# A scalar operand moved from a shared scratch tensor to a tensor of its own

## The chip, the cores and the metric

The kernel runs on one core of a Trainium2 chip. The metric is the device time of one execution in microseconds (us). A core has five engines that run side by side: TensorE (PE, with its weight loads listed apart as PEld), VectorE (DVE), ScalarE (ACT), GpSimd (POOL) and SyncE (SP, which here issues the weight transfers and the stores of the output).

## The reference, cut to what matters

The model is a trunk of two layers over 256 tokens of width 2048, all in float32. Every layer ends both of its halves with a layer norm of a weighted residual, so there are four such norms, and the last of them is the output:

```
def _layernorm(x, w, b):
    mu = jnp.mean(xf, axis=-1, keepdims=True)
    var = jnp.mean(jnp.square(xf - mu), axis=-1, keepdims=True)
    y = (xf - mu) * lax.rsqrt(var + LN_EPS)
    return (y * w + b).astype(x.dtype)
...
for layer in range(2):
    mixed = rwkv7_time_mix(h) if layer == 0 else moba_attention(h)
    h = _layernorm(ALPHA * h + mixed, ln1_w[layer], ln1_b[layer])
    h = _layernorm(ALPHA * h + _swiglu(h, ...), ln2_w[layer], ln2_b[layer])
    if layer == 0:
        k_pad, v_pad, k_mean = _shared_kv(h, kv_w_k, kv_w_v)
return h
```

The reciprocal square root of each norm is what the change touches.

## The kernel before, in words

**Matrix products.** Each float32 weight matrix is streamed from memory in chunks of 256 x 512 values into a ring of four slots, `raw` (SyncE, L296). ScalarE rounds a chunk to `whi` (L950), VectorE writes the rest, `raw - whi`, to `wlo` (L1236, and L1509 in the projections that end in a residual). The activations are held as such a pair too: `ahi` and `alo`, or `hThi` and `hTlo` in the down projections. TensorE makes three products for each piece, at L494 to L496 and in the last block of a projection at L519 to L521: the activation piece (128 x 128) is the stationary operand that is loaded as weights, and the chunk of the ring is the moving one.

**The layer norms.** 256 tokens are two tiles of 128, t = 0 and t = 1. A projection that ends in a residual (`wo`, `down0`, `ao`, `down1`) is made in four blocks of 512 columns. In its last block TensorE finishes tile 0 first, so that VectorE can norm tile 0 while TensorE does tile 1. The function `last_block` does this for one tile: it adds the residual (L1530), takes the block's statistics (L1539), joins those of the four blocks to mean and variance in `mv` (L1540), and makes the reciprocal square root in `rstd` with a first guess from the bits of the float and three Newton steps. All of this works on one value for each token, [128, 1] operands: `x`, the variance plus epsilon, in `var`; `hx`, minus half of it; `y0`, the guess, in `rstd`; and `q`, a scratch value. Before the change both `q` and `hx` are columns of one scratch tensor, `small` of 32 columns: `q` is column t, `hx` is column 2 + t. A `then(...)` around an instruction makes VectorE wait until it has completed. The instruction that writes `hx` (L1543) has no such wait behind it; it signals `split_done` instead, except in the last norm. `hx` is read three times, as the second of the two [128, 1] scalars of L1550.

Eight tiles go through `last_block`: two in each of four norms. After it, `centred` subtracts the mean and multiplies with `rstd` (L1556), and TensorE transposes the result (L842) as the input of the next projection, whose first three chunks it makes at once from the unsplit weights (L852). In the last norm VectorE does the rest itself (L1671, L1676), and SyncE stores each block of 512 columns of the output (L353).

**Where tensors lie.** The tensors are placed in a partition's memory one after another in the order of their declarations, each start rounded up to a multiple of 32 bytes. `raw` starts at byte 16512, `whi`, `wlo`, `ident`, `mixT`, `lnT`, `stats`, `mv`, `var`, `rstd` follow, and `small` starts at byte 67360 with 128 bytes. Behind it come `gsm`, `nsmall`, `idle`, then `ahi` (and under the same bytes `a2t`) at 67904, `alo` at 84288, `big` at 100672 (and under the same bytes `common`, then `hThi` and `hTlo`), and at the end `bsum` and `asm`. `rec` in the profile is `rec2`, which lies under `whi` and `wlo`. Within `big`, the recurrence's tile `XS` starts 96 bytes behind a multiple of 64, since the small tile `PC` of 96 bytes is placed ahead of it; the neighbouring tiles `XT` start at multiples of 64.

Of the kernel before, what the change touches and what calls it, by code (L numbers as in the profile page):

```python
# [29 lines left out]
P = 128  # L30
D = 2048
T = 256
TT = T // P
# [96 lines left out]
def trunk(nc, x, rows, rwkv_rows, lora, w, consts, ln_rows, y):  # L130
    with ExitStack() as ctx:
# [3 lines left out]
        def sb(name, shape, dt=F32, stack=ctx):  # L135
            return stack.enter_context(nc.sbuf_tensor(name, shape, dt))
# [12 lines left out]
        var = sb("var", [P, TT])  # L149
        rstd = sb("rstd", [P, TT])  # L150
        small = sb("small", [P, 32])
        gsm = sb("gsm", [P, 5, 8])
        nsmall = sb("nsmall", [P, 48])
        idle = sb("idle", [P, 10])
# [1049 lines left out]
        def _(dve):  # L1204
# [3 lines left out]
            def then(ins):  # L1208

                step.up(ins)  # L1210
                dve.wait_ge(dve_step, step.now())
# [310 lines left out]
            def last_block(c0, kt, n, t):  # L1522

                c_next = c0 + NJ * kt // KC
                cs = slice((NJ - 1) * NB, NJ * NB)
                if t == 0:
                    dve.wait_ge(tile_done, n + 1)
                else:
                    dve.wait_ge(chunk_used, c_next)
                ins = V.scalar_tensor_tensor(out=Zn[:, t, cs], in0=H[:, t, cs], scalar=ALPHA, in1=ps[:, 2 + t, :], op0=ALU.mult, op1=ALU.add)  # L1530
                if t == 0 and c_next == CHUNKS:
                    then(ins)
                elif t == 0:
                    ins.then_inc(split_done, 1)
                    dve.wait_ge(split_done, c_next + 1)
                else:
                    ins.then_inc(bank_free[1], 1)
                    dve.wait_ge(bank_free[1], (c_jobs[n] + NJ - 1) // 2 + 2)
                then(V.bn_stats(stats[:, t, NJ - 1, :], Zn[:, t, cs]))  # L1539
                then(V.bn_aggr(mv[:, t, :], stats[:, t]))  # L1540
                I32 = mybir.dt.int32
                x, hx, y0, q = (m[:, t:t + 1] for m in (var, small[:, TT:2 * TT], rstd, small))
                ins = V.tensor_scalar(hx, mv[:, t, 1:2], LN_EPS, -0.5, ALU.add, ALU.mult)  # L1543
                if c_next < CHUNKS:
                    ins.then_inc(split_done, 1)
                then(V.tensor_scalar(x, mv[:, t, 1:2], LN_EPS, None, ALU.add))
                then(V.tensor_scalar(q.bitcast(I32), x.bitcast(I32), 1, None, ALU.logical_shift_right))
                then(V.tensor_scalar(y0.bitcast(I32), q.bitcast(I32), -1.0, float(0x5F3759DF), ALU.mult, ALU.add))
                for _ in range(3):
                    then(V.tensor_scalar(q, y0, y0, hx, ALU.mult, ALU.mult))  # L1550
                    then(V.scalar_tensor_tensor(out=y0, in0=q, scalar=1.5, in1=y0, op0=ALU.add, op1=ALU.mult))
# [13 lines left out]
            def norm(n, c_prev, kt, c0):  # L1565

                for t in range(TT):
                    last_block(c_prev, kt, n, t)
                    for b in range(NJ):
                        centred(t, b)  # L1570
                split_act(n, PLAIN)
                split_lo(c0 + PLAIN, 1, PLAIN)
                for g in range(PLAIN + 1, CJ):
                    split_act(n, g)
                split_lo(c0 + RING, 1)
                dve.wait_ge(chunk_used, c0 + PLAIN)
                for g in range(PLAIN):
                    split_act(n, g)
# [88 lines left out]
            for t in range(TT):  # L1667
                last_block(PH["down1"][0], FT, 3, t)
                for b in range(NJ):
                    cs = slice(b * NB, (b + 1) * NB)  # L1670
                    V.scalar_tensor_tensor(out=Zn[:, t, cs], in0=Zn[:, t, cs], scalar=mv[:, t, 0:1], in1=wb_last[:, 0, cs],  # L1671
                                           op0=ALU.subtract, op1=ALU.mult).then_inc(xhat_done, 1)
                for b in range(NJ):
                    cs = slice(b * NB, (b + 1) * NB)
                    dve.wait_ge(xhat_done, (3 * TT + t) * NJ + b + 1)
                    V.scalar_tensor_tensor(out=H[:, t, cs], in0=Zn[:, t, cs], scalar=rstd[:, t:t + 1], in1=wb_last[:, 1, cs],  # L1676
                                           op0=ALU.mult, op1=ALU.add).then_inc(h_done, 1)
# [31 lines left out]
```

## Time and profile before

| | us |
|---|---|
| median of 3 runs (2677.53 to 2678.38) | 2677.69 |
| the profiled execution | 2677.53 |
| span of its profile | 2675.7 |
| what lies around the span | 1.83 |

The profile is that of one execution. Busy times are sums over an engine's instructions; a chain of waits is the work that ended last, followed back from the end. A row of a group of instructions gives its line in the kernel, the engine, the operation, the tensor that is written and those that are read, the shapes, the count, the busy time with the mean of one in ns, and the idle time before them.

### The profile page before, as it was taken

To read this page: it belongs to the slowest core of one execution; us is meant where nothing else is said; L and a number is where in the kernel's file an instruction comes from. 1 tells how busy PE (TensorE), PEld (TensorE's weight loads), DVE (VectorE), ACT (ScalarE), POOL (GpSimd) and SP (SyncE) were. 2 spreads that over 40 slices of the span, in tenths; PEclk is the share of its full clock that TensorE was granted. 3 is DMA by queue.
4 is the path that set the end of the run, shared out by engine and by line. 5 is a ranking of instruction groups with operands and counts; after the bars stand their busy time and mean duration, and the time that the engine had idled before them with its cause. 6 is when DMAs were issued, how large, how long until landed. Compare 5 with 4: busy or idle time off the path is not lost.

```text
span 2675.7 us, 39424 instructions
## 1 busy us (share of the span) xinstructions
PE 2507.8 (94%) x15342; PEld 2045.2 (76%) x15342; DVE 1446.1 (54%) x1738; ACT 1086.0 (41%) x1326; POOL 139.3 (5%) x187
## 2 busy tenths in 40 slices
PE   7999968878999999999999999969999999999997
PEld 5877757766788888887888788857788888887886
DVE  4555976665664444444445644454754444444455
ACT  3444435432444444443333444443444444443332
POOL 1000024430000000000000000010000000000000
PEclk9999979889999999999999999989999999999999
DMA  5555710044466666665665666614566666666664
GB/s 176 166 172 167 216 29 8 14 137 145 150 199 189 186 189 187 188 185 160 191 194 178 210 190 191 193 55 143 155 197 188 188 188 184 189 185 194 191 190 133
DMA packets 219155, 440.75 MB, mean 165 GB/s; under 512 B 13216, under 2 KB 13248, under 8 KB 217824
## 3 DMA queue, kind: packets, MB, share of 16 engines
q1 hardware_dynamic: 214400, 413.19, 51.5%
q0 software_dynamic: 4640, 25.92, 3.5%
q8 instruction: 85, 1.39, 0.2%
q14 instruction: 30, 0.25, 0.0%
HBM read 436.96 MB, written 2.10 MB: 164 GB/s over the span
## 4 chain that ended last, share of the span: by engine, by line
PE 85%; DVE 9%; issue 2%; ACT 2%; DMA 1%; POOL 1%; DVEq 0%; ACTq 0%; POOLq 0%
PE ps L494 25%; PE ps L496 25%; PE ps L495 25%; DVE wlo L1236 2%; PE ps L694 1%; PE ps L880 1%; PE ps L684 1%; PE ps L704 1%; PE ps L852 1%; PE ps L581 1%; DVE rec L1376 1%; DVE alo L1563 1%; DMA big<-lora_a 1%; PE ps L599 1%; PE ps L588 1%
## 5 line engine op out<-in xcount | busy, mean ns | idle before, releaser
L950 ACT CAST whi<-raw 128x1024 fp32r<-128x1024 f32 x772 | 809.3, 1050 | 1234.4 <-PE ps L496 1159.6
L1236 DVE TENSOR_TENSOR wlo<-raw,whi 128x1024 fp32r<-128x1024 f32 x551 | 672.3, 1226 | 676.6 <-ACT whi L950 676.0
L494 PE MATMUL ps<-whi,ahi 128*128 128x512 f32 x2364 | 937.1, 396 | 29.0 <-DVE wlo L1236 12.5
L496 PE MATMUL ps<-whi,alo 128*128 128x512 f32 x2364 | 928.7, 393 | 0.0
L495 PE MATMUL ps<-wlo,ahi 128*128 128x512 f32 x2364 | 925.3, 391 | 0.0
L494 PEld LDWEIGHTS ps<-whi,ahi 128*128 128x128 f32 x2364 | 446.3, 189 | 130.2 <-issue 35.3
L496 PEld LDWEIGHTS ps<-whi,alo 128*128 128x128 f32 x2364 | 445.9, 189 | 101.9
L495 PEld LDWEIGHTS ps<-wlo,ahi 128*128 128x128 f32 x2364 | 446.1, 189 | 97.2 <-issue 0.7
L1509 DVE TENSOR_TENSOR wlo<-raw,whi 128x1024 fp32r<-128x1024 f32 x224 | 274.0, 1224 | 321.4 <-ACT whi L950 321.3
L494 PE MATMUL ps<-whi,hThi 128*128 128x512 f32 x672 | 264.4, 393 | 5.1 <-DVE hTlo L1613 5.1
L495 PE MATMUL ps<-wlo,hThi 128*128 128x512 f32 x672 | 266.0, 396 | 0.0
L496 PE MATMUL ps<-whi,hTlo 128*128 128x512 f32 x672 | 264.6, 394 | 0.0
L494 PEld LDWEIGHTS ps<-whi,hThi 128*128 128x128 f32 x672 | 127.5, 190 | 35.1 <-issue 5.8
L495 PEld LDWEIGHTS ps<-wlo,hThi 128*128 128x128 f32 x672 | 127.5, 190 | 27.6
L496 PEld LDWEIGHTS ps<-whi,hTlo 128*128 128x128 f32 x672 | 127.4, 190 | 27.1
L1126 ACT ACTIVATE a2t<-ps,lnT 128x128 f32<-128x128 f32 x96 | 34.2, 495 | 33.5 <-PE ps L842 33.5
L449 POOL DMA_DIRECT2D big<-ln_rows x3 | 1.7, 573 | 856.7 <-PE ps L521 836.2
L1376 DVE TENSOR_TENSOR rec<-ps,big 128x512 f32<-128x512 f32 x40 | 27.6, 690 | 33.5 <-PE ps L684 32.8
L1250 DVE SCALAR_TENSOR_TENSOR big<-big,mixT 128x256 f32<-128x256 f32 x96 | 40.0, 482 | 0.7
L1382 DVE STREAM_TRANSPOSE rec<-ps 128x512 f32<-128x512 f32 x32 | 22.9, 715 | 31.4 <-PE ps L694 30.9
L1613 DVE TENSOR_TENSOR hTlo<-ps,hThi 128x1024 f32 (+1 forms) x22 | 26.9, 1225 | 21.1 <-ACT hThi L1145 21.1
L694 PE MATMUL ps<-big,rec 64*64 64x64 f32 x960 | 32.7, 234 | 4.7 <-DVE rec L1376 3.9
(286 smaller groups left out, 1669.1 us busy)
## 6 DMA issues: line engine op xcount, KB each, us to landing
raw<-w_gate SPq DMA_DIRECT2D x176, 512.0 KB, 3.7
raw<-w_up SPq DMA_DIRECT2D x176, 512.0 KB, 3.7
raw<-w_down SPq DMA_DIRECT2D x176, 512.0 KB, 3.7
raw<-w_k SPq DMA_DIRECT2D x32, 512.0 KB, 4.2
raw<-w_r SPq DMA_DIRECT2D x32, 512.0 KB, 4.2
raw<-w_v SPq DMA_DIRECT2D x32, 512.0 KB, 4.5
raw<-w_o SPq DMA_DIRECT2D x32, 512.0 KB, 4.4
raw<-kv_k SPq DMA_DIRECT2D x32, 512.0 KB, 4.4
```

Source lines behind the costliest of these rows:

```text
L494: mm(o, hi[:, k, tok], whi[:, s, k2, :], start=(k == 0), stop=False)
L495: mm(o, hi[:, k, tok], wlo[:, s, k2, :], start=False, stop=False)
L496: last = mm(o, lo[:, k, tok], whi[:, s, k2, :], start=False, stop=(k == kt - 1))
L581: last = mm(ps[0:LR, 4 + n, 0:T], m[:, k, :], mx[:, k, :], start=(k == 0), stop=(k == KT - 1))
L694: quarters(lambda j, h, t, a, u, v: mm(ps[u, 2 + a, half(j)], Z[v, a, half(j)], XS[v, half(j)] if a else XT[g % 2][v, 0, half(j)], start=T ...
L950: nc.scalar.copy(whi[:, s], raw[:, s]).then_inc(hi_done, 1)
L1126: ins = A(hF[:, k, t * P:(t + 1) * P], ps[:, 4 + b, k2 * P:(k2 + 1) * P], ACT.Identity, scale=lnT[:, (n * 2) * KT + k:(n * 2) * KT + k + 1 ...
L1236: V.tensor_tensor(wlo[:, s], raw[:, s], whi[:, s].bitcast(F32), ALU.subtract).then_inc(split_done, 1)
L1250: return V.scalar_tensor_tensor(out=out, in0=xxT[:, k], scalar=mixT[:, m * KT + k:m * KT + k + 1], in1=xT[:, k, 1:T + 1], op0=ALU.mult, op ...
L1376: V.tensor_tensor(Z.rearrange("p l (j c) -> p l j c", c=CHUNK), ps[:, 0:2, 0:4 * CHUNK].rearrange("p l (j c) -> p l j c", c=CHUNK), mask_l ...
L1509: V.tensor_tensor(wlo[:, s], raw[:, s], whi[:, s].bitcast(F32), ALU.subtract).then_inc(split_done, 1)
L1613: V.tensor_tensor(hTlo[:, f0, :], ps[:, 4:6, :].rearrange("p a (k t) -> p (a k) t", k=2), hThi[:, f0, :].bitcast(F32), ALU.subtract).then_ ...
```

## The change

One tensor of two columns, `half_var`, is declared behind `small`, and `hx` becomes a column of it instead of column 2 + t of `small`. No instruction is added, taken away or reordered, and no wait changes. `half_var` has 8 bytes and so takes 32: it lies at byte 67488, where `gsm` was, and each tensor declared behind it starts 32 bytes later.

```diff
         small = sb("small", [P, 32])
+        half_var = sb("half_var", [P, TT])
         gsm = sb("gsm", [P, 5, 8])
...
-                x, hx, y0, q = (m[:, t:t + 1] for m in (var, small[:, TT:2 * TT], rstd, small))
+                x, hx, y0, q = (m[:, t:t + 1] for m in (var, half_var, rstd, small))
```

## Rows read from the trace of the kernel before

**Rows 1.** The page: shares of the chain of work that ended last.

```profile
PE 85%; DVE 9%; issue 2%; ACT 2%; DMA 1%; POOL 1%; DVEq 0%; ACTq 0%; POOLq 0%
```

**Rows 2.** Stretches: length; each engine's busy us (instructions); TensorE clock, DMA share, GB/s.

```profile
735.00:1490.00 755.00, 745.64 (x3276) 607.65 (x3276) 379.57 (x347) 307.12 (x317) 1.07 (x2) 0.99 0.63 187
2650.00:2675.70 25.70, 9.37 (x41) 7.34 (x40) 18.40 (x43) 0.00 (x0) 0.00 (x0) 0.74 0.24 82
```

**Rows 3.** The chain of waits in the last 20 us: first and last of six such pieces.

```profile
2656.36 0.28 DVE small L1550
...
2666.55 0.28 DVE small L1550
```

**Rows 4.** VectorE in order of time, last tile of last norm: start us, length us.

```profile
2664.91 0.15 DVE L1543 TENSOR_SCALAR small<-mv 128x1 f32<-128x1 f32 x1
2664.99 0.14 DVE L1546 TENSOR_SCALAR var<-mv 128x1 f32<-128x1 f32 x1
2665.16 0.15 DVE L1547 TENSOR_SCALAR small<-var 128x1 int32<-128x1 int32 x1
2665.35 0.15 DVE L1548 TENSOR_SCALAR rstd<-small 128x1 int32<-128x1 int32 x1
```

**Rows 5.** VectorE in order of time in the first norm, `centred` of both tiles.

```profile
711.28 1.92 DVE L1556 TENSOR_SCALAR common<-common,mv,rstd 128x512 f32<-128x512 f32 x4
...
717.00 1.92 DVE L1556 TENSOR_SCALAR common<-common,mv,rstd 128x512 f32<-128x512 f32 x4
```

**Rows 6.** The chain of waits there: start us, length us, what.

```profile
712.85 1.75 PE ps L842 x16
...
714.93 5.39 PE ps L852 x12
720.32 0.45 PE ps L842 x4
```

**Rows 7.** VectorE's groups of instructions, shapes kept apart.

```profile
L1550 DVE TENSOR_SCALAR small<-rstd,small 128x1 f32<-128x1 f32 x24 | 6.6, 273 | 0.9
L1547 DVE TENSOR_SCALAR small<-var 128x1 int32<-128x1 int32 x8 | 1.2, 154 | 0.3
L1556 DVE TENSOR_SCALAR common<-common,mv,rstd 128x512 f32<-128x512 f32 x24 | 11.5, 543 | 0.2
L1562 DVE CAST ahi<-a2t 128x512 fp32r<-128x512 f32 x24 | 10.1, 421 | 14.5 <-ACT a2t L1126 14.5
```

**Rows 8.** The page: TensorE's weight loads at line 494.

```profile
L494 PEld LDWEIGHTS ps<-whi,ahi 128*128 128x128 f32 x2364 | 446.3, 189 | 130.2 <-issue 35.3
...
L494 PEld LDWEIGHTS ps<-whi,hThi 128*128 128x128 f32 x672 | 127.5, 190 | 35.1 <-issue 5.8
```

**Rows 9.** Line 694, products on `XS` and `XT`: ns min/median/max, first and last start.

```profile
L694 PE MATMUL ps<-big,rec x960: 213/218/366, 381.0 to 577.0; 64*64 64x64 f32 x192
L694 PE MATMUL ps<-rec x320: 216/218/366, 381.0 to 557.7; 64*64 64x64 f32 x160
```

**Rows 10.** ScalarE's copies into `XS` (L1036) and `XT` (L1043).

```profile
L1036 ACT COPY big<-ps 64x256 f32<-64x256 f32 x32 | 11.8, 370 | 0.4
L1043 ACT COPY rec<-ps 128x256 f32<-128x256 f32 x16 | 6.0, 373 | 25.4 <-DVE rec L1382 25.4
```

**Rows 11.** Line 1250, reading `xT` at steps of 1028 bytes.

```profile
L1250 DVE SCALAR_TENSOR_TENSOR big<-big,mixT x96: 475/480/491, 17.7 to 265.2; 128x256 f32<-128x256 f32 x96
```

**Rows 12.** The chain of waits, whole span: its two transfers among the longest pieces.

```profile
7.05 14.12 DMA big<-lora_a
...
266.55 7.31 DMA big<-rwkv_rows
```

**Rows 13.** Page: DMA queues: packets, MB, share of 16 engines.

```profile
q1 hardware_dynamic: 214400, 413.19, 51.5%
q0 software_dynamic: 4640, 25.92, 3.5%
```

**Rows 14.** The output's stores, from the answer on their tensor.

```profile
DMA to landing us min/median/max: 2.4/2.7/2.8
```

## The prediction

> **What bounds the kernel now.** I read the page first. The chain of work that ended last is TensorE for 85% of the span and VectorE for 9% [rows 1], so a change on VectorE counts only where the chain runs through it. Next the stretches. In 735 to 1490 us, products without a norm between them, TensorE is busy for 745.64 of 755 us with 3276 products, 228 ns each, and VectorE for half of the time [rows 2]. There nothing that VectorE does for 0.1 us is seen. The last 25.7 us are the opposite: TensorE works for 9.37 us in them and VectorE for 18.40. The chain of waits shows why: it runs through L1550 six times, three Newton steps for each of the two tiles of the last norm [rows 3]. In the three other norms the same instructions have a cover. In the first norm, tile 0's `centred` starts at 711.28 and its first of four pieces is done after a quarter of 1.92 us, at 711.76 [rows 5]; TensorE turns to it only at 712.85, when it has finished tile 1 [rows 6], so 1.09 us are free. Tile 1's first piece is done at 717.48 [rows 5], and TensorE takes it at 720.32, behind the 12 products of L852 [rows 6]: 2.84 us are free. The reader is to see that of eight passes through `last_block` only two lie on the path.
>
> **The change part by part.** Nothing is added or removed: the same instructions on the same engines, in the same order, with the same waits, semaphores and transfers. What changes is addresses, of two sorts. I cost every one of them at nothing, and bound each from the rows.
>
> (a) *Where `hx` lies, as it is read.* L1550 reads `y0` as its tensor, `y0` again as its first scalar and `hx` as its second, and writes `q`. It takes 273 ns, where L1547, of the same size with a constant in place of the scalars, takes 154 [rows 7]: 119 ns more. Before the change `hx` lies in the tensor that L1550 writes, 8 bytes from the value. Is the 119 ns the price of that closeness? L1556 says no: it reads two [128, 1] scalars, `mv` and `rstd`, neither of which lies in the tensor that it writes, and takes 543 ns, where the cast of L1562, which has the same 512 values a partition and no scalar, takes 421 [rows 7]. That is 122 ns more. So two scalars cost about 120 ns wherever they lie; 122 - 119 = 3 ns is what the closeness could be worth, and in six instructions on the path that is 0.02 us. Expected: nothing. Bounds: if in spite of that row the closeness were the whole price, moving `hx` away would give back 6 x 0.119 = 0.71 us on the path, and 24 x 0.119 = 2.86 us if none of the 24 had a cover. In the other direction a further scalar's price, half of 119 ns, six times, is a loss of 0.36 us; if the pair's price doubled, it would be 0.71 us and 2.86 us in the same way.
>
> The Trainium skill (Advanced Engine Details and Errata, SBUF Cachelines) speaks against this change: it gives lines of 16 bytes, with full speed when following accesses hit the same line and a penalty when they don't. The four values of `q` and `hx` fill just one such line before (byte 67360 is 4210 x 16) and two after. By that rule L1550 would get slower, and the time would be that of the rival of a dearer L1550 below.
>
> (b) *Where `hx` lies, as it is written.* L1543 has no wait behind it, and L1546 starts 0.08 us after it, although it lasts 0.15; where a wait stands between, the next instruction starts after 0.19 (L1547 to L1548) [rows 4]. Both orders write different tensors before and after, so I expect the same. If the new address held L1546 back, each pass would lose 0.11 us, 0.22 us on the path for two passes and 0.88 for eight. If the cover of (a) and (b) were gone in all eight, the sum would be 3.74 us, still only 0.14%.
>
> (c) *The shift by 32 bytes.* This is the part with reach. `ahi`, `alo`, `hThi` and `hTlo`, all of `big` and `common` start at multiples of 64 before, and 32 bytes beyond one after. The ring `raw`, `whi`, `wlo` lies ahead of `small` and stays, and with it the moving operand of nearly all products, ScalarE's L950 and VectorE's L1236 and L1509. What moves is TensorE's stationary operand. Its load takes 189 ns from `ahi` and 190 from `hThi` [rows 8] and lies beside the 228 ns of a product, so it has 38 ns to grow in before any product is late. Rows on operands that are 32 bytes off already: `XS` is read as the moving operand at L694, and 640 of the 960 products of the group `big` read it, the other 320 `XT`; the median of this group is 218 ns, like that of the group `rec`, which reads only `XT` at multiples of 64 [rows 9]. ScalarE writes 256 values into `XS` in 370 ns and 256 into `XT` in 373 [rows 10]. VectorE's L1250 reads `xT` at steps of 1028 bytes, thus from 16 different places against a 64-byte grid, and its 96 instructions lie between 475 and 491 ns [rows 11]. No row shows a weight load from such a place; the nearest are those of the moving operand, and I take no change. The bound there is the rival below.
>
> (d) *Transfers.* The queue that fills the ring carries 413.19 MB [rows 13], and the ring doesn't move. GpSimd's 25.92 MB do go to shifted places, nearly all. On the chain are 14.12 us of loading `lora_a` and 7.31 of the broadcast rows [rows 12], and at the end the last store, 2.7 us [rows 14]. I expect them unchanged. The Trainium skill (DMA: Bandwidth & Descriptors, How a descriptor splits into AXI transactions) has a read start at the multiple of 256 bytes below it: for the stores' pieces of 2048 bytes, 64 bytes beyond one before and 96 after, that is 67 beats of 32 bytes in place of 66. By it the last store would take an estimated 0.04 us more; no run so far shows it.
>
> The sum is 0, made against the profiled execution's 2677.53 us (2675.7 of span and 1.83 around it), which is 0.16 below the median. The forecast is the median, 2677.7 us. I call 0.2% of it, 5.4 us, what a measurement of this kernel can tell from no change.
>
> **The rivals.** *The load of a shifted operand gets dearer (slower).* The projections' three products are made with 9108 loads of moved operands at L494 to L496 alone: three lines, each with 2364 on `ahi` or `alo` and 672 on `hThi` or `hTlo` [rows 8]. Up to 38 ns each is hidden. Beyond, each ns costs 9.1 us, so the rival decides from 38.6 ns, a load that takes a fifth longer; if a load took a quarter longer, 47 ns, the time would be 2677.7 + 9 x 9.1 = 2760 us. For it: no row has a load from such an address. Against it: rows 9 to 11, three engines that don't care. Chance 2%.
>
> *Transfers into shifted places get slower.* 14.12 + 7.31 us of them are on the chain. A loss of 5.4 us needs all of it to take 25% longer; then the time is 2683. Nothing in the rows speaks for it but that GpSimd's transfers are the ones that moved. Chance 1%.
>
> *`hx` apart from `q` makes L1550 or L1543 cheaper.* If all 119 ns vanished, 2677.0 us, by the six on the path. L1556 speaks against it. Chance 3%; it stays inside 0.2% even at 2.86 us. *`hx` apart from `q` makes L1550 dearer,* since it then reads and writes small values in two places of memory instead of one: 2678.4 us at a doubled price of the scalars, also inside 0.2%. The 3 ns between L1556 and L1550 [rows 7] are all that speaks for it. Chance 4%. (It is what the Trainium skill's section SBUF Cachelines would lead to.) Faster by over 0.2% would need a fraction of a ns gained in each of the 15,342 products, or some 5.4 us in the norms, where L1550 takes 6.6 us in all: chance 2%.
>
> **How the numbers follow.** My forecast of no effect in any part has 88%, the two small rivals 3 and 4, the two that slow it 3, and what would make it faster 2. Same: 88 + 3 + 4 = 95%; slower 3%; faster 2%. The range is the bound of (a) without any cover on both sides, 2.86 us, which also holds the spread of the runs of 0.85: 2674.8 to 2680.6.
>
> **What would show it right or wrong.** In the changed kernel's profile L1550 should stay within 5 ns of 273, L1546 should start 0.07 to 0.08 us behind L1543, the loads of L494 should take 188 to 191 ns with products at 228 ns, and L694 should show 218 for both groups. With 250 ns or 300 at L1550, (a) is wrong but the time is not. The prediction is wrong if a load passes 228 ns, or if the stretch from 735 to 1490 us changes its length by more than 2 us.

## The result, and the profile after

The change makes the kernel slower. The median of the four runs beside the kernel before is 2715.93 us against 2678.03, a ratio of 1.0138 with a 95% interval of 1.0118 to 1.0158. One of the four took 13648.72 us for a cause that nothing here shows; it counts as a slow run, and the ratio is that of the fast ones. The forecast was 2677.7 us and no change. The profiled execution took 2719.42 us with a span of 2717.6.

The part that the change edits looks as forecast. These are VectorE's groups of instructions of the changed kernel (its lines are one higher), to be held against [rows 7]:

```profile
L1551 DVE TENSOR_SCALAR small<-rstd,half_var 128x1 f32<-128x1 f32 x24 | 6.6, 273 | 0.9
L1548 DVE TENSOR_SCALAR small<-var 128x1 int32<-128x1 int32 x8 | 1.2, 154 | 0.3
L1557 DVE TENSOR_SCALAR common<-common,mv,rstd 128x512 f32<-128x512 f32 x24 | 11.5, 542 | 0.2
```

And this is its VectorE in order of time in the last tile of the last norm, against [rows 4]:

```profile
2706.83 0.15 DVE L1544 TENSOR_SCALAR half_var<-mv 128x1 f32<-128x1 f32 x1
2706.91 0.14 DVE L1547 TENSOR_SCALAR var<-mv 128x1 f32<-128x1 f32 x1
2707.08 0.15 DVE L1548 TENSOR_SCALAR small<-var 128x1 int32<-128x1 int32 x1
```

The instruction that reads `hx` from its new place takes the same 273 ns, and the one behind the write of `hx` still starts 0.08 us later. The loss is elsewhere. TensorE's busy time is 41.5 us up, VectorE's and ScalarE's are within 1.3 us of what they were, and the weight loads are no longer than before (188 ns against 189). The first line of the page, before:

```profile
PE 2507.8 (94%) x15342; PEld 2045.2 (76%) x15342; DVE 1446.1 (54%) x1738; ACT 1086.0 (41%) x1326; POOL 139.3 (5%) x187
```

The page of the changed kernel, with its weight loads, to be held against [rows 8]:

```profile
PE 2549.3 (94%) x15342; PEld 2042.7 (75%) x15342; DVE 1445.9 (53%) x1738; ACT 1084.7 (40%) x1326; POOL 139.3 (5%) x187
...
L495 PEld LDWEIGHTS ps<-whi,ahi 128*128 128x128 f32 x2364 | 444.3, 188 | 145.9 <-issue 37.0
...
L495 PEld LDWEIGHTS ps<-whi,hThi 128*128 128x128 f32 x672 | 127.2, 189 | 37.0 <-issue 5.9
```

A stretch with no norm in it shows it best. Of each kernel this is the row for 800 to 1200 us, with TensorE busy for all of it; first before, then after:

```profile
800.00:1200.00 400.00, 400.00 (x1787) 329.07 (x1786) 195.74 (x161) 166.88 (x161) 0.00 (x0) 1.00 0.64 187
```

```profile
800.00:1200.00 400.00, 400.00 (x1750) 322.36 (x1749) 192.84 (x159) 162.41 (x158) 0.00 (x0) 1.00 0.64 184
```

In the same 400 us TensorE starts 37 instructions fewer, 29 of them products and 8 short transposes that stand between them, at the full granted clock (1.00) in both. TensorE in order of time in the changed kernel (start us, length us):

```profile
899.94 0.40 PE L495 MATMUL ps<-whi,ahi 128*128 128x512 f32 x1
900.17 0.39 PE L496 MATMUL ps<-wlo,ahi 128*128 128x512 f32 x1
900.41 0.40 PE L497 MATMUL ps<-whi,alo 128*128 128x512 f32 x1
900.64 0.39 PE L495 MATMUL ps<-whi,ahi 128*128 128x512 f32 x1
```

Three products take 0.70 us from start to start. I call the time between two starts the pitch. Over all products at L494 to L496 and L519 to L521 whose successor starts within 260 ns, the trace's starts give a mean pitch of 228.99 ns before and 233.33 after. There are 9300 such products (9108, and 192 in the last blocks), so 4.34 ns each is 40.4 us; the span grew by 41.9. The match is a rough one: not all of the 9300 follow right upon each other, and 3.3 us of the growth lie in the recurrence, which has none of these products; the run e1_end below, with the distances of the kernel before, has a recurrence as long as that. From the first statistics join of the first norm to that of the second there are 755.1 us before and 768.6 after, from that of the third norm to that of the fourth 755.1 and 768.5, and from the first tile to the second of the last norm 9.2 in both.

Products of other forms have not changed. Their lengths are in the groups of TensorE's instructions below, first before, then after; the median time from one start to the next is the same too, 429 ns at L852 and 216 at L588 in both kernels.

```profile
L852 PE MATMUL ps<-raw,a2t 128*128 128x512 f32 x72 | 32.4, 600 | 1.9 <-issue 1.0 <-ACT a2t L1126 0.9
L588 PE MATMUL ps<-big 128*128 128x256 f32 x64 | 14.0, 379 | 0.0
```

```profile
L853 PE MATMUL ps<-raw,a2t 128*128 128x512 f32 x72 | 32.4, 600 | 1.9 <-issue 1.0 <-ACT a2t L1127 0.9
L589 PE MATMUL ps<-big 128*128 128x256 f32 x64 | 14.0, 379 | 0.0
```

### The profile page after: what moved, and what is told of

The parts are those of the page before. It is cut to its first block, busy times and chain, and to the rows that moved or that the text cites. A ratio compares the mean times of both kernels' runs of the same rounds, so it can differ in the third digit from the quotient of the medians.

```text
span 2717.6 us, 39424 instructions
## 1 busy us (share of the span) xinstructions
PE 2549.3 (94%) x15342; PEld 2042.7 (75%) x15342; DVE 1445.9 (53%) x1738; ACT 1084.7 (40%) x1326; POOL 139.3 (5%) x187
## 4 chain that ended last, share of the span: by engine, by line
PE 86%; DVE 9%; issue 2%; ACT 2%; DMA 1%; POOL 1%; DVEq 0%; ACTq 0%; SPq 0%; POOLq 0%
PE ps L495 25%; PE ps L496 25%; PE ps L497 25%; DVE wlo L1237 2%; PE ps L881 1%; PE ps L685 1%; PE ps L695 1%; PE ps L705 1%; PE ps L582 1%; PE ps L853 1%; DVE rec L1377 1%; DMA big<-lora_a 1%; DVE alo L1564 1%; PE ps L600 1%; PE ps L589 1%
## 5 line engine op out<-in xcount | busy, mean ns | idle before, releaser
L495 PE MATMUL ps<-whi,ahi 128*128 128x512 f32 x2364 | 940.7, 398 | 29.7 <-DVE wlo L1237 12.9
L496 PE MATMUL ps<-wlo,ahi 128*128 128x512 f32 x2364 | 935.5, 396 | 0.0
L496 PEld LDWEIGHTS ps<-wlo,ahi 128*128 128x128 f32 x2364 | 444.5, 188 | 107.2 <-issue 0.7
L496 PE MATMUL ps<-wlo,hThi 128*128 128x512 f32 x672 | 267.3, 398 | 0.0
L496 PEld LDWEIGHTS ps<-wlo,hThi 128*128 128x128 f32 x672 | 127.1, 189 | 31.3
```

The lines of the kernel that those rows point to most:

```text
L495: mm(o, hi[:, k, tok], whi[:, s, k2, :], start=(k == 0), stop=False)
L496: mm(o, hi[:, k, tok], wlo[:, s, k2, :], start=False, stop=False)
```

## The experiments

**Where `hx` lies, or the shift of the others?** Four kernels ran on one chip. The first keeps `half_var` but declares it last:

```diff
-        half_var = sb("half_var", [P, TT])
...
         asm = [sb(f"asm{n}", [P, 3, 2, 2]) for n in range(2)]
+        half_var = sb("half_var", [P, TT])
```

> hx is a column of half_var as in the change, but half_var is declared last, so that every other tensor lies where it lay before. If the new 38 us come from the 32 bytes by which the change shifts the tensors behind small (theory A), the pitch of the three products is 229 ns again, the stretch of pure products is as before and the time is 2678 us. If they come from where hx itself lies, as it is read or written (theory B), the pitch is 233 ns and the time 2716 us.

Measured: 2683.74 us, a ratio to before of 1.0009 (0.9994 to 1.0024), 1786 instructions in the 400 us, a pitch of 229.5 ns. The new place of `hx` costs nothing that can be measured.

The 229.5 instead of 229.0 has its source in one stretch, between the second norm and the third. There the same products, on operands at the same bytes as before, run at 233.3 ns for more than 200 us and then go back to 228.9. The row for 1520 to 1720 us, of the kernel before and of this run:

```profile
1520.00:1720.00 200.00, 200.00 (x875) 164.13 (x874) 89.94 (x73) 84.23 (x82) 4.54 (x6) 1.00 0.66 192
```

```profile
1520.00:1720.00 200.00, 200.00 (x859) 162.01 (x858) 88.32 (x72) 82.82 (x80) 4.54 (x6) 1.00 0.64 191
```

So one layout can run in more than one rhythm. (The kernel before has such a stretch too, at 233.4 ns for some 20 us from 260 us on.) This comes back below. The second kernel leaves `hx` in `small` and shifts the rest:

```diff
         small = sb("small", [P, 32])
+        gap = sb("gap", [P, 8])
```

> hx stays in small as before; an unused tensor of 32 bytes is declared behind small, so that all tensors behind it are shifted as in the change. Theory A (the shift): 2716 us, pitch 233 ns. Theory B (hx's own place): 2678 us, pitch 229 ns.

Measured: 2719.25 us, ratio 1.0147 (1.0119 to 1.0176), pitch 233.33 ns. The same row of this kernel:

```profile
800.00:1200.00 400.00, 400.00 (x1750) 322.31 (x1749) 192.87 (x159) 162.38 (x158) 0.00 (x0) 1.00 0.63 184
```

Theory B, `hx`'s own place, fell; theory A, the shift, stood: an unused tensor of 32 bytes does all that the change does. The third doubles the gap:

```diff
+        gap = sb("gap", [P, 16])
```

> The same with an unused tensor of 64 bytes: the tensors behind small start at multiples of 64 again, 64 bytes later than before. If the place against a 64-byte grid decides (theory A1), 2678 us and a pitch of 229 ns. If any other distance to the ring of weight chunks decides, or a coarser grid of 128 bytes (theory A2), some other pitch, lower or higher, with 9.1 us for each ns of it.

Measured: 2656.12 us, ratio 0.992 (0.989 to 0.9951): faster than the kernel before. The pitch is 226.83 ns, and the row is

```profile
800.00:1200.00 400.00, 400.00 (x1803) 331.89 (x1802) 197.62 (x162) 168.42 (x162) 0.00 (x0) 1.00 0.65 189
```

So it isn't a grid of 64 bytes. 9300 x (228.99 - 226.83) = 20 us; the span fell by 21.0. The fourth shifts both operands:

```diff
+        gap = sb("gap", [P, 8])
         raw = sb("raw", [P, RING, KC, NB])
```

> The unused tensor of 32 bytes is declared ahead of raw, so that the ring (the moving operand) and the activations (the stationary operand) are both shifted by 32 bytes and keep their distance. If the stationary operand's own place against the grid decides, 2716 us and 233 ns. If the distance between the two operands decides, 2678 us and 229 ns. If the moving operand's place matters too, more than 2716 us.

Measured: 2679.77 us, ratio 1.0008 (0.9993 to 1.0024), pitch 228.95 ns. `ahi` lies at the same byte as in the changed kernel, and the loss is gone. What counts is the distance between the two operands, not the place of one.

**At which distances?** D is the start of the activations' tensors minus that of the ring's, taken modulo 512 at first and modulo 256 once the pattern is seen to repeat, and it is the same for `ahi`, `alo`, `hThi` and `hTlo` as long as no gap stands between them (they are multiples of 512 bytes apart, as are `whi` and `wlo`). With gaps ahead of `ahi` (`gap1`) and ahead of `big` (`gap2`) one run gives two values of D. The diff is that of s1; s2 has 48 and 32 columns in place of 24 and 8, s3 64 and 56. Theory A is now that the product's own two operands decide, theory C that something else in the layout does, such as the traffic of other engines. Each of the runs s1 to s4 is a single execution, so its time has no interval; the pitches are means over thousands of products of it.

```diff
         idle = sb("idle", [P, 10])
+        gap1 = sb("gap1", [P, 24])
...
         alo = sb("alo", [P, KT, T], F32R)
+        gap2 = sb("gap2", [P, 8])
```

> D is the distance from the ring's tensors to the stationary operand's, modulo 512: 192 before, 224 in the change, 256 with 64 bytes of gap (pitches 229.0, 233.3, 226.8 ns). Here ahi and alo move by 96 bytes (D = 288), hThi and hTlo by 128 (D = 320). If the product's own operands decide (theory A), the products on ahi and alo and those on hThi and hTlo have two different pitches in one run. If something else in the layout decides (theory C), both have the same. If only an odd or even multiple of 32 matters (theory A1), ahi stands near 233 ns and hThi at 227 to 229.

Measured: 2709.69 us (before, on this chip, 2677.44). Pitch 233.3 ns on `ahi` and `alo`, 233.3 on `hThi` and `hTlo`. Both of its distances are dear ones, so this run can't tell theory A from theory C. It does end theory A1, by which odd multiples of 32 alone are dear: D = 320 is an even one. The time is 6 us under the changed kernel's at the same pitch; most of that lies in the recurrence (193.8 us from its first transpose on VectorE to its last, 200.4 in the changed kernel, 197.2 in the one before), and wasn't followed up.

> ahi and alo move by 192 bytes (D = 384), hThi and hTlo by 320 (D = 0). Theory A: each group has the pitch of its own D. A grid of 64 alone gives 227 to 229 ns for both; a coarser one gives two pitches, one of them perhaps under 226.8.

Measured: 2692.1 us; 232.6 ns on `ahi` and `alo` (D = 384), 226.7 on `hThi` and `hTlo` (D = 0). Two pitches in one run: theory A stands, theory C, by which both groups have one pitch, fell as it was stated. Its rows for a stretch of products on `ahi` (the first, with 24 short transposes in it) and one on `hThi`:

```profile
800.00:950.00 150.00, 150.00 (x660) 121.97 (x659) 71.79 (x59) 61.14 (x59) 0.00 (x0) 1.00 0.64 184
1250.00:1400.00 150.00, 150.00 (x663) 124.24 (x663) 72.05 (x61) 58.05 (x56) 0.00 (x0) 1.00 0.64 193
```

In the kernel before, with D = 192 for both, the second stretch has fewer instructions; in the changed one fewer still:

```profile
1250.00:1400.00 150.00, 150.00 (x657) 123.08 (x656) 71.47 (x61) 57.08 (x55) 0.00 (x0) 1.00 0.64 192
```

```profile
1250.00:1400.00 150.00, 150.00 (x645) 120.49 (x644) 70.67 (x60) 55.54 (x53) 0.00 (x0) 1.00 0.63 189
```

> ahi and alo move by 256 bytes (D = 448), hThi and hTlo by 480 (D = 160, an odd multiple of 32). Theory A: two pitches; if the pattern repeats every 256 bytes, ahi has 229.0 ns as before. If all odd multiples of 32 are dear, hThi has 233 ns.

Measured: 2684.14 us; 229.0 ns on `ahi` and `alo` (D = 448), just as at D = 192, so the pattern repeats every 256 bytes; 233.3 on `hThi` and `hTlo` (D = 160).

The fourth reaches that D = 160 from the other side, by 32 bytes ahead of `raw` and 480 ahead of `ahi`:

> The ring moves by 32 bytes, the stationary operands by 512, a full turn, so D = 160 comes from moving the ring and not the activations. If the distance alone decides, the pitch is that of hThi in the run with 480 bytes (s3), for both groups. If the stationary operand's own place decides, it is 229.0 ns, as before; if the moving one's place alone costs, it is something else.

Measured: 2718.48 us, pitch 233.3 ns in both groups, as at D = 160 in s3. So it is the distance again, by whichever operand it is made.

**The change with another shift, and the operands one by one.**

```diff
-        half_var = sb("half_var", [P, TT])
+        half_var = sb("half_var", [P, 16])
```

> The change as it was, hx in half_var, but half_var has 16 columns (64 bytes) instead of 2, so that the tensors behind it move by 64 bytes instead of 32 and D, the distance from the ring to the activations modulo 256, is 0. If D alone decides, the pitch is 226.8 ns and the time 2656 us, 0.8% less than before. If hx's own place cost anything, it would lie above the 2656 us of the run with the gap of 64 bytes (e3).

Measured in five rounds: 2654.98 us, ratio 0.9907 (0.9891 to 0.9922), pitch 226.82 ns. This is the change with a wider `half_var`, and it beats both kernels. Its groups show `hx` in its new tensor, at the old price, and its row the fast pitch:

```profile
L1551 DVE TENSOR_SCALAR small<-rstd,half_var 128x1 f32<-128x1 f32 x24 | 6.6, 273 | 0.9
...
800.00:1200.00 400.00, 400.00 (x1802) 331.92 (x1801) 197.59 (x163) 168.40 (x162) 0.00 (x0) 1.00 0.62 189
```

The next three are single executions again. The first places all tensors on multiples of 16 bytes, with gaps that give the distances named:

```diff
-            return stack.enter_context(nc.sbuf_tensor(name, shape, dt))
+            return stack.enter_context(nc.sbuf_tensor(name, shape, dt, align_bytes=16))
...
+        gap1 = sb("gap1", [P, 56])
...
+        gap2 = sb("gap2", [P, 44])
```

> Tensors are placed on multiples of 16 instead of 32. ahi and alo have D = 96, the class that is still missing; hThi and hTlo have D = 16, half a step of what the 32-byte placement allows. If each step of 32 away from 0 other than 192 is dear, ahi has 233 ns. For hThi: 233 ns if only an exact 0 is cheap, 227 ns if the grain is 32 bytes or more.

Measured: 2665.11 us; 227.6 ns on `ahi` and `alo` (D = 96), where I had expected 233, and 226.7 on `hThi` and `hTlo` (D = 16). The 227.6 is a mean of more than one rhythm: from one interruption by transposes to the next the products at D = 96 run at 226.7 ns or at 230.0, as in these two neighbouring stretches:

```profile
880.00:920.00 40.00, 40.00 (x176) 32.75 (x175) 19.20 (x17) 15.72 (x15) 0.00 (x0) 1.00 0.60 185
925.00:965.00 40.00, 40.00 (x178) 33.12 (x177) 19.80 (x17) 15.74 (x15) 0.00 (x0) 1.00 0.62 190
```

```diff
         whi = sb("whi", [P, RING, KC, NB], F32R)
+        gap3 = sb("gap3", [P, 8])
         wlo = sb("wlo", [P, RING, KC, NB], F32R)
...
         idle = sb("idle", [P, 10])
+        gap1 = sb("gap1", [P, 8])
```

> A gap of 32 bytes between whi and wlo, and 32 more behind idle: the activations have D = 0 to whi and D = 224 to wlo. If what decides is the distance between a stationary operand's load and the moving operand that is read beside it, only the products that stream wlo (L495), a third of all, are dear: their pitch is 233 ns, the others' 226.8, the mean 229 ns and the time 2677 us. If the distance to the ring as a whole, or the other engines' traffic on it, decides, all three lines have one pitch.

Measured: 2709.25 us. The products that stream `wlo` have the longest pitch, 235.7 ns on `ahi`, but those on `whi` are slower than 226.8 too: 231.9 with `ahi`, 229.9 with `alo`. The mean is 232.5, not 229: the idea that each of the three products is late by itself, and the mean is their sum over three, fell.

```diff
         idle = sb("idle", [P, 10])
+        gap1 = sb("gap1", [P, 16])
...
-            a2t = sb("a2t", [P, 8192], stack=early)
+            a2t = sb("a2t", [P, 8200], stack=early)
...
+        gap3 = sb("gap3", [P, 8])
         alo = sb("alo", [P, KT, T], F32R)
...
-        hF = carve(a2t, KT * T, KT, T)
+        hF = carve(a2t, KT * T + 8, KT, T)
```

> ahi has D = 0, alo, hThi and hTlo have D = 32. In the products on ahi and alo one of three is dear. If a product's pitch is set by its own stationary operand, it is L496, which uses alo (the kernel's L497 or so, behind new lines). If it is set by the load of the next product's stationary operand, which runs beside it, it is L495, whose successor uses alo. The products on hThi and hTlo have 233 ns. The time is near 2690 us.

Measured: 2714.81 us. The longest pitch, 238.9 ns, is that of the product `wlo` with `ahi`, whose successor uses `alo`; the product that uses `alo` itself has 228.4, the one behind it 232.4. This fits a product being late when the *next* one's stationary operand, which is loaded meanwhile, lies badly to its own moving operand, and so does the `wlo` product of t3. It is not the whole: the other two products of t4, whose loads lie at D = 0 to them, are slower than 226.8 as well. The mean of 233.3 is again more than a third of the way from 226.8, and the time 25 us over the expected one.

**TensorE alone.** What was left was whether TensorE's own two reads are enough. The kernel's core, for each block of 48 products:

```python
mm(o, hi, whi, start=(k == 0), stop=False)
mm(o, hi, wlo, start=False, stop=False)
last = mm(o, lo, whi, start=False, stop=(k == 7))
```

> A kernel of its own that leaves out the whole model: TensorE alone makes 80 blocks of 48 products in the order and shape of the projections (128 x 128 stationary, 128 x 512 moving), on constant data, with nothing else running beside them. The first 32 blocks step D, the distance from the moving to the stationary tensors modulo 512, from 0 to 496 in steps of 16, the next 32 go back, eight more move alo alone by 0 to 224, and eight move wlo alone. If the loss is TensorE's own, from its two operands (theory A), the pitches are those of the full kernel: 226.8 ns at D = 0, 233.3 at 32 and 64, 232.6 at 128, 233.3 at 160, 229.0 at 192, 233.3 at 224, the same 256 bytes further on. If ScalarE's and VectorE's traffic on the ring has a part in it (theory C), all 32 have one pitch. The blocks with alo or wlo moved alone should give the 233.3 and 232.5 ns means of t4 (alo by 32) and t3 (wlo by 32); if they give 229, a third of the way, the extra in the full kernel comes from elsewhere.

Measured (the whole takes 914.36 us). The mean pitch of each block without its first six products, in ns, worked out from the trace's starts:

```
D mod 256      0     16     32     48     64     80     96    112
upwards      226.7  226.7  233.4  233.3  233.3  232.0  234.3  233.3
downwards    226.7  233.3  233.4  233.3  233.3  232.1  234.3  233.3
D mod 256    128    144    160    176    192    208    224    240
upwards      233.4  233.4  233.4  230.0  228.9  233.3  233.3  226.7
downwards    232.5  233.3  233.4  230.0  228.8  231.9  233.3  226.7
alo alone off by    32: 233.4    64: 231.0    96: 232.5   128: 231.1
                   160: 233.3   192: 231.1   224: 231.1
wlo alone off by    32: 231.8    64: 232.2    96: 231.1   128: 233.4
                   160: 232.2   192: 229.2   224: 231.0
```

The upward row is the second turn, D = 256 to 496; the first turn gave the same (its very first block holds TensorE's start and is left out). The last rows shift `alo` alone or `wlo` alone: by 32 bytes this gives 233.4 and 231.8 ns, where t4 had 233.3 and t3 232.5. TensorE in order of time in the block at D = 256, with nothing else at work:

```profile
193.09 0.39 PE L64 MATMUL ps<-mov,stat 128*128 128x512 f32 x1
193.31 0.39 PE L65 MATMUL ps<-mov,stat 128*128 128x512 f32 x1
193.54 0.39 PE L66 MATMUL ps<-mov,stat 128*128 128x512 f32 x1
193.76 0.39 PE L64 MATMUL ps<-mov,stat 128*128 128x512 f32 x1
```

Three starts are 0.67 us apart here, 0.70 in the changed kernel. The map has the full kernel's values at D = 0, 32, 64, 128, 160, 192 and 224 within 0.2 ns (at 128 the downward one), with no work on any other engine. So TensorE's own two operands are enough, and theory C isn't needed for the loss. D = 96 is the exception: 234.3 ns in the map, 226.7 and 230.0 in t2. Together with e1_end this says that the distance doesn't fix the pitch alone. At D = 0 and 32, the distances of the fast and of the changed kernel, every trace keeps to one rhythm, 226.7 and 233.3 ns, but for the products just behind an interruption.

## Why the prediction was wrong

- **(a) and (b), where `hx` lies, were right.** L1551 stayed at 273 ns, the start behind L1544 at 0.08 us, and the kernel with `half_var` declared last has a ratio of 1.0009. The comparison with L1556 that put the 119 ns down to the two scalars, and not to the closeness, held. The dearer L1550 of the rivals didn't come either.
- **(d), the transfers, was right** as far as the time goes: the output's stores land in 2.8 us at the median (2.7 before), rounded figures that can't tell whether the estimated 0.04 us is there, and `lora_a` takes 14.42 us on the chain (14.12). The broadcast rows take 7.83 us (7.31). Both lie within what the runs here show for the same transfers, 12.9 to 14.4 us and 7.3 to 8.2, at shifted places and at unshifted ones.
- **(c), the shift by 32 bytes, failed,** in the step "it has 38 ns to grow in before any product is late". I priced the address by the *length of the load* and took the 38 ns between it and the pitch as its cover. The load didn't grow at all (188 ns). The pitch grew, by 4.3 ns, with the load still some 45 ns shorter than it. The 228 ns [rows 2] was busy time over all instructions of the stretch, short transposes included; the products' own pitch before is 229.0. And it wasn't a fixed cost to be read off and set against the load: it held already 2.2 ns that came from the operands' distance, as the 226.8 ns at D = 0 show.
- **The rows chosen as evidence couldn't show it.** L694 [rows 9] is of another form, 64 columns by 64, and lengths were compared there, not pitches; the groups of ScalarE and VectorE [rows 10, 11] read one place at a time. They bear on the place of one operand, and e4 shows that this place indeed costs nothing. The question that wasn't asked is the distance between the two operands that one engine reads at once.
- **The rival with the right place had the wrong mechanism.** It named the shifted stationary operand and the number of products, and its 9.1 us for each ns is about right (41.9 us over 4.34 ns is 9.7, with the recurrence's 3.3 us in it; without them, 8.9). But it let the cost begin at 38 ns of a longer load, and so got 2% and 2760 us.
- **What stood for wrong did tell it:** the two stretches between norms, one of which holds the 735 to 1490 us that were named, grew by 13.4 us each, where 2 us were the limit.

The Trainium skill (SBUF — State Buffer, Who interferes with whom) lists TensorE's two read ports, one for the moving operand and one for the weight load, as independent, and says that TensorE never waits on anyone. These runs don't bear out the first half in time: in the kernel of TensorE alone the pitch goes from 226.7 to 234.3 ns with nothing changed but the distance between the two operands. As the load got no longer, only a comparison of pitches shows it.

What stays open: why these distances, and what picks the rhythm. The map isn't a simple grid (192 costs 2.2 ns over D = 0, 64 costs 6.6), a single misplaced tensor of four costs more than its share, and D = 16 keeps the pitch of the block ahead of it, 226.7 behind D = 0 and 233.3 behind D = 32. D = 96 gave 226.7 and 230.0 ns in the full kernel and 234.3 in the map, and D = 192 gave 228.9 and, in one stretch of e1_end, 233.3; what sets one or the other wasn't followed up. It may have a part in the 16 us by which 19 executions of the kernel before differ (2670.9 to 2686.8), which isn't shown. That the two reads get in each other's way in some part of the memory that repeats every 256 bytes fits the dependence on D, but it is argued, not shown.

## What to carry to other kernels

An edit that allocates anything moves all tensors declared behind it, and where TensorE streams one tensor while it loads another, the time can change without an instruction changed: here by 1.4% up for 32 bytes and by 0.9% down for 64. So a new small tensor is declared last, or padded so that the tensors behind it keep their distance modulo 256; and a comparison of two kernels whose layouts differ is first made with the layout held equal. Where a kernel is bound by products like these, it is worth trying to put the stationary and the moving tensors a multiple of 256 bytes apart: here that gave the 0.9%. Other shapes and types weren't tried. And when a cost is said to be hidden, check it on the spacing of the instructions that set the pace, not on the length of the one that is hidden.

## What the runs showed that I had not expected

- The pitch of a product of 128 x 512 with a freshly loaded 128 x 128 operand is 226.7 to 234.3 ns, by the distance of its two operands modulo 256 above all, at the full granted clock, with the load at 188 to 190 ns throughout.
- The rhythm has a memory: at D = 16, 128 and 208 the same products run at 226.7 or 233.3, 233.4 or 232.5, 233.3 or 231.9 ns, by the distance that the products ahead of them had. In the full kernel one layout held 228.9 and 233.3 ns in one execution (D = 192), and another 226.7 and 230.0 (D = 96).
- Within the mean the pitches form a pattern that repeats: 229, 232 and 226 ns in turn before, 231 and 236 in turn at D = 64.
